# First expert job unrolled in front of the loop, its tokens gathered by TensorE, and the last job's results spread by TensorE, in a two-layer hybrid decoder with a mixture of experts

## The reference

```python
x = x + gate_m * rms_norm(hybrid_mixer(h, ...), norm_mix_post[i])
h = rms_norm(x, norm_ffn_pre[i]) * (1.0 + scale_f) + shift_f
logits = h @ w_router
top_logits, top_idx = lax.top_k(logits, 2)
gates = softmax(top_logits)
y[t] = sum over its two experts e of  gates * ((silu(h[t] @ w1[e]) * (h[t] @ w3[e])) @ w2[e])
x = x + gate_f * rms_norm(y, norm_ffn_post[i])
```

## Time and profile before

| | |
|---|---|
| median of 3 runs | 1883.56 us (1880.21 to 1887.18) |
| the profiled execution's own time | 1881.89 us |
| its span, first to last instruction | 1879.9 us |
| mean granted TensorE clock | 0.96 |
| busy, share of the span | PE 93%, VectorE 79%, ScalarE 59%, GpSimd 5% |
| moved by DMA | 550 MB, 293 GB/s in the mean |

### The profile page before, as it was taken

One profiled execution on the slowest core, in us unless ns is written; L12 is line 12 of the kernel. 1 busy time (PEld: TensorE's weight loads), 2 busy tenths in 40 slices (PEclk: granted clock), 3 DMA queues, 4 the chain that ended last, 5 costly groups with the idle time before them and its releaser, 6 DMA issues.

```text
span 1879.9 us, 24937 instructions
## 1 busy us (share of the span) xinstructions
PE 1743.2 (93%) x8953; PEld 1473.0 (78%) x8953; DVE 1483.6 (79%) x1435; ACT 1103.3 (59%) x971; POOL 93.3 (5%) x102
## 2 busy tenths in 40 slices
PE   5999869999899885999999999999999999999994
PEld 5988759899788774887887888878878788788883
DVE  4886867888787844888888888888888888888884
ACT  1543522434454433677677686686776767777672
POOL 0000100000000010000100101001001010010101
PEclk9898979999899885999999999999999999999997
DMA  9445647878455641999999999999999999999993
GB/s 311 148 136 179 222 137 246 273 265 291 136 179 180 221 138 67 350 386 355 369 381 350 380 362 354 396 348 372 366 363 386 354 364 385 353 378 362 353 394 119
DMA packets 289668, 550.28 MB, mean 293 GB/s; under 512 B 13366, under 2 KB 113992, under 8 KB 289608
## 3 DMA queue, kind: packets, MB, share of 16 engines
q1 hardware_dynamic: 281328, 533.76, 80.3%
q0 software_dynamic: 3888, 14.16, 2.3%
q10 hardware_dynamic: 4392, 1.57, 0.4%
HBM read 540.55 MB, written 8.91 MB: 292 GB/s over the span
## 4 chain that ended last, share of the span: by engine, by line
PE 52%; issue 39%; DVE 4%; ACT 2%; POOL 1%; ACTq 1%; POOLq 1%; DMA 1%; DVEq 0%
PE ps L1480 17%; PE ps L1481 16%; PE ps L1482 16%; DVE lo_ring L1409 3%; PE ps L1790 1%; ACT stage_hi L940 1%; POOL rstd L684 1%; POOL rstd L675 0%; PE ps L1727 0%; DVE m_act L1415 0%; ACTq L759 0%; DVE a_lo L1419 0%; POOLq L683 0%; ACTq L752 0%; DMA xg<-tokens,xidx 0%
## 5 line engine op out<-in xcount | busy, mean ns | idle before, releaser
L1409 DVE TENSOR_TENSOR lo_ring<-weight_ring,stage_hi 128x2048 fp32r<-128x2048 f32 x378 | 849.3, 2287 | 110.4 <-ACT stage_hi L940 110.2
L940 ACT CAST stage_hi<-weight_ring 128x2048 fp32r<-128x2048 f32 x378 | 705.2, 1912 | 106.4 <-DMA weight_ring<-in_moe_w_dram 99.9
L1480 PE MATMUL ps<-stage_hi,xe_hi 128*128 128x512 f32 x1008 | 406.1, 403 | 8.7 <-DVE lo_ring L1409 8.7
L1481 PE MATMUL ps<-lo_ring,xe_hi 128*128 128x512 f32 x1008 | 397.5, 394 | 0.0
L1482 PE MATMUL ps<-stage_hi,xe_lo 128*128 128x512 f32 x1008 | 396.3, 393 | 0.0
L1049 DVE TENSOR_TENSOR lo_ring<-weight_ring,stage_hi 128x2048 fp32r<-128x2048 f32 x81 | 185.1, 2292 | 80.0 <-ACT stage_hi L797 73.1
L1480 PE MATMUL ps<-h_hi,stage_hi 128*128 128x256 f32 x800 | 237.4, 297 | 8.0 <-DVE h_lo L1012 7.8
L797 ACT CAST stage_hi<-weight_ring 128x2048 fp32r<-128x2048 f32 x81 | 153.7, 1905 | 139.3 <-DMA weight_ring<-in_w_in_dram 62.9
L1481 PE MATMUL ps<-h_lo,stage_hi 128*128 128x256 f32 x800 | 233.0, 291 | 0.0
L1482 PE MATMUL ps<-h_hi,lo_ring 128*128 128x256 f32 x800 | 232.7, 291 | 0.0
L1480 PEld LDWEIGHTS ps<-stage_hi,xe_hi 128*128 128x128 f32 x1008 | 189.9, 188 | 54.6 <-DVE lo_ring L1409 13.0
(11 more groups left out here) (292 smaller groups left out, 1705.9 us busy)
## 6 DMA issues: line engine op xcount, KB each, us to landing
weight_ring<-in_moe_w_dram SPq DMA_DIRECT2D x378, 1024.0 KB, 5.3
weight_ring<-in_w_mod_dram SPq DMA_DIRECT2D x48, 1024.0 KB, 7.8
weight_ring<-in_w_in_dram SPq DMA_DIRECT2D x36, 1024.0 KB, 5.5
weight_ring<-in_ffn_w_dram SPq DMA_DIRECT2D x33, 1024.0 KB, 6.5
weight_ring<-in_w_out_dram SPq DMA_DIRECT2D x12, 1024.0 KB, 5.1
moe_rows<-y_e POOLq DMA_DIRECT2D x10, 512.0 KB, 8.1
moe_rows<-y_moe POOLq DMA_DIRECT2D x3, 512.0 KB, 3.9
x_tok<-in_x_dram SPq DMA_DIRECT2D x1, 1024.0 KB, 10.4
```

The source lines that it names most:

```text
L940: nc.scalar.copy(jst_hi[i % JSTAGES][:], ring[:, n % RING, :]).then_inc(hi_ready, 1)
L1409: nc.vector.tensor_tensor(ring_lo[:, n % RING, :], ring[:, n % RING, :], raw(jst_hi[i % JSTAGES][:]), ALU.subtract).then_inc(lo_ready, 1)
L1480: mm(dst, lh, rh, start=start, stop=False)
L1481: mm(dst, lh, rl, start=False, stop=False)
```

## The change

It moves five things.

1. The last gate row becomes a step of the written list: `("grow", 1, 1)` stands behind `("grow", 1, 0)` ahead of the last w_out slot of layer 1, in banks 6 and 7, and goes to a buffer of its own, `gate_last`.
2. Job 0 is written out in front of the loop on ScalarE, VectorE and PE, and the loops there and on GpSimd begin with job 1. The first two slots of job 0 are split before the tokens are there.
3. The tokens of job 0 aren't fetched: PE multiplies `h_tok`, as the stationary operand, with the marks `sel` of job 0, 16 products of 128 by 128 in float32, into the banks in which the loop's transposes put theirs. The tokens are still stored to DRAM for the later jobs.
4. Only what `select` of job 0 needs is made ahead of it: positions, mask, counts. The job table, the extra columns, the gates and the return rows are made by VectorE inside job 0, one piece at the end of each of the chunks 2 to 5. The gates get a table by job as well (`gatej`). The number of jobs is loaded by the engines behind job 0. The clearing of `y_moe` moves behind the first select, and five blocks of `moe_rows` are cleared with it (three before). Two dummy products and their semaphore `m_dn` go away.
5. The last job's result isn't stored and fetched. GpSimd fetches the returns in the last job, behind the store of the result before it; the last job's rows read zeros there. VectorE sums them into `y_moe` in advance. PE transposes the last job's marks, weighed with the gates, multiplies them with the last result, and VectorE adds that to `y_moe`.

```diff
             if n == 5:
                 s.append(("grow", l, 0))
+                if l:
+                    s.append(("grow", l, 1))
...
-            for k in range(NE + 1, NJOB + 1):
+            cleared = [0] + list(range(NE, NJOB + 1))
+            pool.wait_ge(y_zero, 1)
+            for k in cleared:
                 pool.dma_start(y_rows[k * P:(k + 1) * P, :], y_moe[:, 0, :]).then_inc(rows_cleared, 16)
...
-            with pool.Fori(0, n_jobs) as job:
-                pool.wait_ge(xidx_ready, job + 2)
+            with pool.Fori(1, n_jobs) as job:
+                pool.wait_ge(xidx_ready, job + 1)
...
-            pool.wait_ge(ye_out, n_jobs + 1)
-            pool.dma_start(y_rows[bass.ds(n_jobs * P, P), :], y_e[:]).then_inc(y_kept, 16)
-            pool.wait_ge(y_kept, n_jobs * 16 + 16)
-            nc.gpsimd.tensor_tensor(tick[:], neghalf[:, 0:1], neghalf[:, 0:1], ALU.mult)
+
             pool.wait_ge(rows_ready, 1)
...
+            act.wait_ge(st_used, ND)
+            for i in range(2):
+                split_of(0, i)
             for g in range(4):
                 act.wait_ge(htok_done, g + 1)
...
-            act.wait_ge(grow_done, 2 * DEPTH)
-            act.wait_ge(x_ready, TT * (2 * DEPTH - 1))
-            nc.scalar.copy(gate_row[:], pair(UPB)).then_inc(grow_ready, 1)
+            split_of(0, 2)
+            gathered_hi(0)
             act.wait_ge(r_del, 1)
             nc.scalar.activation(led[:], ldel[:], ACT.Exp).then_inc(r_exp, 1)
...
+            expert(0, True)
+            act.wait_ge(routed, 1)
+            n_jobs = act.value_load(njob[0:1, 0:1], min_val=NE, max_val=NJOB)
+            with act.Fori(1, n_jobs) as job:
+                expert(job, False)
+
+            act.wait_ge(y_free, n_jobs)
             act.wait_ge(st_used, n_jobs * JOB_SLOTS + ND)
-            act.wait_ge(y_free, n_jobs + 1)
-            nc.scalar.copy(y_e[:], pair(YB)).then_inc(ye_out, 1)
+            nc.scalar.copy(y_e[:, 0:512], ps[:, YB, :]).then_inc(ye_half, 1)
...
+            nc.vector.tensor_copy(mskj[:, :, 0:NE], msk[:])
+            split_of(0, 1)
+            dve.wait_ge(pos_done, 1)
+            nc.vector.tensor_copy(posj[:, :, 0:NE], ps[:, RB, 16:16 + TT * NE].rearrange("p (t e) -> p t e", t=TT))
+            nc.vector.tensor_copy(cnts[:], ps[:, RB, 32:32 + NE])
             nc.vector.drain()
...
+            select(0, mskj, 0)
+            nc.vector.memset(y_moe[:], 0.0)
+            nc.vector.drain().then_inc(y_zero, 1)
...
                         split(o + 4)
                         split(o + 5)
+                        if first and ch == 2:
+                            more_jobs()
+                        if first and ch == 3:
+                            more_places()
+                        if first and ch == 4:
+                            gates()
+                        if first and ch == 5:
+                            back_rows()
...
+            expert(0, True)
+            dve.wait_ge(routed, 1)
+            n_jobs = dve.value_load(njob[0:1, 0:1], min_val=NE, max_val=NJOB)
+            with dve.Fori(1, n_jobs) as job:
+                expert(job, False)
+
+            select(n_jobs, gatej, n_jobs - 1)
             for t in range(TT):
                 dve.wait_ge(y_landed[t], 32)
...
+            dve.wait_ge(st_used, n_jobs * JOB_SLOTS + ND)
+            nc.vector.tensor_copy(y_e[:, 512:], ps[:, YB + 1, :]).then_inc(ye_half, 1)
+            dve.wait_ge(sT_done, 1)
+            nc.vector.tensor_copy(selT[:].rearrange("p t n -> p (t n)"), ps[:, IDXB, 0:TT * P]).then_inc(sT_ready, 1)
+            for t in range(TT):
+                dve.wait_ge(back_done, t + 1)
+                nc.vector.tensor_tensor(y_moe[:, t, :], pair(2 * t), y_moe[:, t, :], ALU.add)
                 nc.vector.drain().then_inc(ysub_done, 1)
...
+            pe.wait_ge(htok_h, 4)
+            pe.wait_ge(sel_ready, 1)
+            for g in range(2):
+                for k in range(4):
+                    kt = 4 * g + k
+                    for t in range(TT):
+                        last = mm(ps[:, XB[g], k * P:(k + 1) * P], h_tok[:, t, kt * P:(kt + 1) * P], sel[:, t, :],
+                                  start=(t == 0), stop=(t == TT - 1))
+                last.then_inc(xt_done, 1)
...
+            expert(0)
+            pe.wait_ge(routed, 1)
+            n_jobs = pe.value_load(njob[0:1, 0:1], min_val=NE, max_val=NJOB)
+            with pe.Fori(1, n_jobs) as job:
+                expert(job)
+
+            pe.wait_ge(sel_ready, n_jobs + 2)
+            for t in range(TT):
+                last = nc.tensor.transpose(ps[:, IDXB, t * P:(t + 1) * P], sel[:, t, :], ident[:])
+            last.then_inc(sT_done, 1)
             pe.wait_ge(xh_ready, n_jobs * 2 + 2)
             pe.wait_ge(xl_ready, n_jobs * 2 + 2)
+            pe.wait_ge(sT_ready, 1)
+            pe.wait_ge(ye_half, 2)
+            for t in range(TT):
+                for half in range(2):
+                    last = mm(ps[:, 2 * t + half, :], selT[:, t, :], y_e[:, half * 512:(half + 1) * 512],
+                              start=True, stop=True)
+                last.then_inc(back_done, 1)
```

More of the change, by code:

```diff
@@ L409, in build @@
         dense.close()
-        back = ExitStack()
-        y_back = sb("y_back", [P, TT, 2, D], F32, back)
-        h_tok = sb("h_tok", [P, TT, D], F32, back)
-        back.close()
         m = sb
@@ L472, in norm_bank, with grow_bank @@
             return (0, 1, 4, 5)[g] if (l, s) == (1, 0) else 4 + g
+        def grow_bank(l, i):
+            return 4 if i == 0 else 6 if l else 0
         LGB, RB = 2, 3
@@ L950, in transposed @@
                     nc.scalar.copy(a_hi[:, ch % 2], ps[:, TPB, :].rearrange("p (k n) -> p k n", k=4)).then_inc(m_th, 1)
-                for i in range(3):
-                    split(i)
-                act.wait_ge(st_used, job * JOB_SLOTS + ND)
-                act.wait_ge(y_free, job + 1)
-                nc.scalar.copy(y_e[:], pair(YB)).then_inc(ye_out, 1)
+                if not first:
+                    for i in range(3):
+                        split(i)
+                    act.wait_ge(st_used, job * JOB_SLOTS + ND)
+                    act.wait_ge(y_free, job)
+                    nc.scalar.copy(y_e[:], pair(YB)).then_inc(ye_out, 1)
                 split(3)
@@ L1296, in _, with split_of, select, places @@
                     post_norm(l, i)
-            nc.vector.memset(y_moe[:], 0.0)
+            def split_of(job, i):
+                n = NS + i
+                dve.wait_ge(hi_ready, job * JOB_SLOTS + (ND + i + 1))
+                nc.vector.tensor_tensor(ring_lo[:, n % RING, :], ring[:, n % RING, :], raw(jst_hi[i % JSTAGES][:]),
+                                        ALU.subtract).then_inc(lo_ready, 1)
+            def select(job, table, table_job):
+                for t in range(TT):
+                    one = lambda a: a[:, t, bass.ds(table_job, 1)]
+                    nc.vector.tensor_scalar(sel[:, t, :], iota[:], one(posj), one(table), ALU.is_equal, ALU.mult)
+                nc.vector.drain().then_inc(sel_ready, 1)
+            def places(job):
+                dve.wait_ge(pos_ready, job)
+                nc.vector.tensor_copy(xidx[:], ps[:, IDXB, 0:1]).then_inc(xidx_ready, 1)
+            def gathered_lo(job):
+                for g in range(2):
+                    dve.wait_ge(xh_ready, job * 2 + (g + 1))
+                    nc.vector.tensor_tensor(xe_lo[:, 4 * g:4 * g + 4, :],
+                                            ps[:, XB[g], :].rearrange("p (k n) -> p k n", k=4),
+                                            raw(xe_hi[:, 4 * g:4 * g + 4, :]), ALU.subtract).then_inc(xl_ready, 1)
+            split_of(0, 0)
             dve.wait_ge(lg_done, 1)
@@ L1338, in _ @@
-            nc.vector.tensor_scalar(njf[:], ranki[:, NE - 1:NE], float(NE), None, ALU.add)
-            nc.vector.drain()
-            for k in range(EXTRA):
-                nc.vector.scalar_tensor_tensor(out=ohk[:, k, :], in0=rank[:], scalar=float(k), in1=over[:],
-                                               op0=ALU.is_equal, op1=ALU.mult)
-            nc.vector.drain()
-            nc.vector.tensor_tensor(epick[:], ohk[:], iota[:, 0:NE].unsqueeze(1).to_broadcast([P, EXTRA, NE]), ALU.mult)
@@ L1404, in _, with expert @@
             gathered_lo(0)
-            with dve.Fori(0, n_jobs) as job:
+            def expert(job, first):
                 def split(i):
-                    n = NS + i
-                    dve.wait_ge(hi_ready, job * JOB_SLOTS + (ND + i + 1))
-                    nc.vector.tensor_tensor(ring_lo[:, n % RING, :], ring[:, n % RING, :], raw(jst_hi[i % JSTAGES][:]),
-                                            ALU.subtract).then_inc(lo_ready, 1)
+                    split_of(job, i)
                 def product(ch):
@@ L1420, in transposed @@
                                             ALU.subtract).then_inc(m_tl, 1)
-                for i in range(4):
+                for i in range(2 if first else 0, 4):
```

(17 more changed lines are left out.)

211 lines of the change are left out of this document (105 added, 106 removed).

## The result

The changed kernel takes 1856.82 us in the median of four runs (1855.95 to 1859.94), beside 1884.39 (1880.21 to 1887.18) for the kernel before in the same session: a ratio of 0.9863, 95% interval 0.9843 to 0.9883. It is faster by 27.6 us, or 1.4%. The forecast was 1856.5. The profiled execution of after took 1857.11 us, its span is 1855.3, its mean clock 0.97.

What follows compares the result with a forecast made beforehand. PE was taken to set the pace of the jobs, transfers close behind, so gains lay at both ends: 1881.9 − 18.5 − 1.75 + 2 + 0.3 + 3 − 10.5 = 1856.5 us, range 1850 to 1867.

Steps and rivals of the forecast that it cites:

- The start: From router logits to first expert product: no token fetch, tables later, early splits; first product at 728.45 against 746.92, −18.5 us.
- The gather: TensorE's 32 passes making job 0's tokens at the start, half of them at each clock: 5.75 us, bounds 3.9 and 7.6.
- The gate row: Last gate row's 16 passes, moved from the start to ahead of the last w_out slot, cost 1.95 us there.
- The clock of the first products: Job 0's first nine products run at full clock at once, not half: −1.75 us, bound 0.
- The tables in job 0: VectorE's 7.5 us of table work inside job 0 mostly fits its slack: +2 us, bounds 0 and 7.5.
- Rival A: All 7.5 us of VectorE's table work show in job 0, since it has no lead: 1862 us, chance 0.12.
- The loop's head: Engines load the job count between job 0 and job 1: +0.3 us, bounds 0 and 1.18.
- The last job: Four return fetches, 2.1 MB, delay the weights there, part being absorbed: +3 us, bounds 0 and 5.7.
- Rivals B and C: Last job's fetches cost 5.7 us, nothing absorbed: 1859.2, chance 0.10; or all stalls, tables' included, absorbed: 1851.2, chance 0.08.
- The tail: Behind PE's last product, last result added without store and fetch: first block after 4.3 us, not 14.2; −10.5 us altogether.
- Rival D: Something other than tokens and tables holds the first product, so only the tail gains: 1874.4 us, chance 0.05.
- Rival E: Job 0 written out, then the loop body, wait for seven more instruction packets under weight traffic: slower, 1912 us, chance 0.03.

Runs made afterwards that it cites:

- Experiments 3 to 5: Changed kernel with one part undone each: job 0's tokens fetched again, 1861.37 us; first three splits behind the casts, 1861.35; tables ahead of the first select, 1865.03.
- Experiments 3 and 4: Changed kernel with job 0's tokens fetched from DRAM again, 1861.37 us; and with its first three splits behind the token casts, 1861.35 us.
- experiment 10: `returns_late` with the gates and return rows of job 0 each cut in two and put behind different splits: 1850.49 us, ratio 0.9822.
- tables_front: Changed kernel with job table, extra columns and return rows made ahead of the first select, gates left in job 0: 1865.03 us, ratio 0.9893.
- experiment 7: Changed kernel with the four return fetches spread behind slots 22, 26, 30 and 34 of the last job: 1854.28 us, ratio 0.9853.
- experiment 1: Both kernels unchanged, each profiled a second time: before 1882.99 us, after 1858.07 us.
- returns_late: Changed kernel with the four return fetches behind slots 22, 29, 36 and 38 of the last job: 1851.88 us, ratio 0.9829.

## Why the prediction was right, step by step

**The total is right to 0.3 us by luck.** The forecast took 25.4 us off the profiled 1881.9. The medians differ by 27.6 us, and the three stretches by 27.8. The gain was thus forecast 2.2 us too small, and the start of the sum lay 2.5 us below the median of before (1884.39). The two cancel. What stands on its own is the path and the sign and size of each term, below.

**The start: −18.5 forecast, −17.4 in position, −20.6 as the change's own.** The path is the one that was written down: logits, transposes, positions, select, gather, casts. Measured from the norm's transposes to the first product it takes 22.9 us, forecast 24.9. Of the 2 us 1.7 are the router passes (5.29 us for 7.00), where I had taken the clock of before, half throughout. The gather took 5.97 for 5.75: the clock rose at 726.6, so some 20 of its 32 passes ran at half clock, not 16. The gate row cost 3.73 − 1.95 = 1.78 us for 1.95. Against this better start stands the gate rows' place, 3.2 us late and mostly by chance. Experiments 3 to 5 price three parts: the tables 6.1 us, the tokens 5.0, the early splits 5.1. They can't be added: each run undoes one part while the others stay, and the half clock behind an idle PE is counted both in the tokens and in the splits.

**The clock of the first products: −1.75 forecast.** In job 0, over the same work, the finely cut version takes 117.02 us, where before took 118.86: −1.84. Experiments 3 and 4 bring the half clock back and lose 2.1 and 1.8 up to the first w2.

**The tables in job 0: +2 forecast, +1.5 measured** (experiment 10). The four pieces take 2.0, 1.3, 2.2 and 2.3 us in the trace. Behind those of chunks 2 and 3 PE doesn't wait, behind the other two it waited 0.44 and 0.60, and their chunks grew by 0.69 and 0.83. Rival A put the price at 7.5, and the slack per chunk was the right argument against it. That a piece is free up to a fixed slack is not shown: 2.0 us passed and 2.2 did not, and in `tables_front` the same gates at the same place made PE wait 0.81 us for 0.44, with no piece ahead of them.

**The loop's head: +0.3 forecast, 0 measured.** From the w2 of job 0's last chunk into job 1 (848.02 to 868.07) PE takes 20.05 us, and 20.04 in before. The load of the job count that the engines now make there doesn't show: the lower bound.

**The last job: +3 forecast, +3.3 measured.** Rivals B and C were its bounds, 5.7 and 0. The value between was right for this code, but the reason given, that a fixed 2.8 us are absorbed, does not hold. What is absorbed depends on when the bytes are asked for: the same 2.1 MB cost 3.2 us in a burst, 2.4 at some 11 us apart, nothing with two 20 us apart and two behind the last load. The Trainium skill, "DMA: Bandwidth & Descriptors", section on queues, rings and completion order, lets each DMA engine alternate between queues. The last job agrees in kind, the weights came late right behind the fetches; but a stream halved for the whole fetch would have cost 5.7, and the stream had room (395 GB/s in experiment 7, beside 363 ahead of the fetches). How much the filled ring slots absorbed wasn't measured.

**The tail: −10.5 forecast, −10.24 measured,** with two errors that cancel in part. The spread was priced as four passes at 0.235 us. It is four float32 products, which the trace shows as eight passes of 0.46 each, at the full clock (1.00 from 1839.4): 3.67 us, of which the first half, 2.0, lies ahead of the first add, where I had counted all four passes as 0.94. The price stood in the rows: in the earlier trace rows 128 columns of float32 take 0.12 us a pass at full clock, so 512 take 0.49, and in the earlier trace rows the two dummy products of 512 columns are four passes and 2.11 us. The 0.235 was that of products of rounded operands. Against it the copies went side by side on ScalarE and VectorE, and the add began on the first block while the second was still spread.

**Rival D** (the gain doesn't come) is out by the start itself, 20.6 us shorter. **Rival E** (the body waits for its code) is out by the queues. Instruction packets from 729 to 855, in job 0:

```profile
q8 instruction: 5, 0.08, 0.3%
q14 instruction: 3, 0.02, 0.0%
```

From 855 to 975, the loop's first pass, there are four and one more, and none in the two jobs behind it. So the code is read twice, as E said, and no wait of PE belongs to them: from 829.13 to 1792.10 it has none above 0.3 us, and `late_and_fine`, which reads its code in the same way, has none in job 0 either.

**What stays open:** why the clock of the mixer and of the router passes differs between profiles, which moves the first product by up to 5 us; whether the 1.7 us of the router passes belong to the moved gate row, since all ten profiles with it have them and three of the four without it don't; and whether some of the +3.2 us of the gate rows' place is the change's after all. By the estimate of experiment 1 that is 0.8 us, give or take 1.2.

## What to carry to other kernels

A step that fills an idle stretch ahead of a busy one is worth its own time and the half clock that it spares the work behind it; here that was 1.8 to 2.1 us on top of 3.1 to 3.5. Side work on an engine with slack did best in small pieces: two of 2.2 and 2.3 us cost 1.5 us together, and nothing once each was cut in two. Transfers beside a stream that keeps the DMA engines busy can be placed by its spare rate or behind its last load; here 0.5 MB at 20 us apart and two such behind the last load were free, and 11 us apart mostly moved the wait. And compare kernels by stretches between instants of the program: the place where the first one begins moved by 5 us between profiles, the stretches of one kernel by 0.3. Where a total agrees to a fraction of that chance, it is luck, and the terms have to be checked one by one.

## What the runs showed of the hardware that was not expected

- Ten profiles of kernels with the same program up to the gate rows reach them between 689.37 and 694.88 us. The granted clock over the same 14 us of the mixer was 0.63 to 0.77 in them, and it explains the place only in part (experiment 1).
- A float32 product of 512 columns takes 0.92 us at full clock (two passes of 0.46), a single product of rounded operands 0.23.
- An indirect fetch of 0.5 MB occupies GpSimd for 0.94 to 0.99 us in some places and for 2.1 to 3.0 in others. It doesn't go by the load: in `returns_late` it was 2.72 at 1781.28 and 0.96 at 1821.19, both with the DMA engines at 410 GB/s, and 2.21 at 1829.62, where they moved 4. In the tail of before, with 187 GB/s in the mean, it was 0.94 to 0.99 four times. The profile calls its spans on GpSimd rough, and why they differ wasn't tried.
- The DMA engines moved up to 410 to 417 GB/s for short stretches of the last job, where a job in the middle moves 369 in the mean.
